# Weighting of the second map moved to GpSimd, and late value units and gate banks rearranged, in a two-block attention kernel

## The chip, the cores and the metric

The kernel runs on one core of a Trainium2 chip. The metric is the device time of one execution in microseconds, taken as the median of several runs. TensorE is called PE in the profile, VectorE DVE, ScalarE ACT, GpSimd POOL, SyncE SP.

## The reference, cut to what matters

Two transformer blocks run one after the other on 256 latent tokens of width 1024. The first block has a Fourier mixer layer, then a differential attention layer (8 heads of two maps, 512 keys: 256 latent and 256 context), each with a feed-forward part. The second adds 16 meta tokens and runs multi-head latent attention (MLA, 8 heads, 272 keys) and neighbourhood attention (NA, 16 heads) side by side, each times a silu gate, then one output projection.

```
differential:  p = softmax(q1 k1^T) - lam * softmax(q2 k2^T);   o = rmsnorm(p v) * gain;   x += gate * (o @ w_out)
MLA:           p = softmax(scale * (qn kn^T + qp kp^T));        y_mla = (p v) * silu(g_mla)
NA:            p = softmax(scale * q k_win^T + bias);           y_na  = (p v) * silu(g_na)
out:           x += concat(y_mla, y_na) @ w_out_2
```

## The kernel before, in words

Everything is fp32, kept exact to about fp32 by splitting each operand of a projection into a rounded part and a rest; a projection tile is then three fp32r matmuls per 128 rows of the contraction (`product`, lines 528 to 530, and for token-major tiles lines 966 to 968). SP loads weights by slabs of two halves; ACT rounds each half (line 503), DVE forms the rest (line 510), four halves fit. PE walks all projections as **units**: a unit is one PSUM bank, 24 matmuls for a contraction of 1024 and 6 for 256. A head unit is then squared by ACT, summed over partitions by PE (`unit_sum`) in bank 3 or 4, inverted by ACT (lines 1027 and 1029) and scaled by DVE (line 1128), with a rotation where needed (1143 to 1146); a token unit is copied out by ACT (line 1085); a meta unit (line 953) is added up by DVE (1107 to 1110). Units of the deep phases go round banks 0, 1, 2, 5, 6, 7 and are finished two units later; gate units go round banks 0, 1, 2. Each engine has its own instruction order written out by hand, and in-order waits on semaphores join them.

**Differential attention** (`att_pe`, `att_act`, `att_dve`) has 16 steps (8 heads, two query halves). Its first steps follow the last two token units of the phase: one is run before step 0, one in iteration 2. In iteration i, PE runs the scores of step i (line 1223, two maps, banks 0 to 3 in turn), in odd iterations the value product of a head (1238), in even ones the sum of squares of a head (1260), then the transposes of step i-2 (1252). ACT runs the two exponentials of step i (1277), copies the transposes of step i-2 out (1287), squares a head (1299) or forms its inverse root (1304, 1306). DVE takes the maxima of step i (1371), the reciprocals of the sums of step i-1 (1347), scales the second map (1353) and adds the scaled first one (1355), and in odd iterations scales a head (1382). POOL only rounds and splits the finished heads (`heads_split`, 1335 and 1337). Four parts of the output projection (15 matmuls each, contraction tiles 0 to 4 of output tiles 0 to 3) are run by PE after the transposes of iterations 17, 17, 19 and 20; the rest follows in `outproj_pe`, whose output tile 0 needs the last head's split (line 1328) for its contraction tile 7.

**MLA attention** (`mla_pe`, `mla_act`, `mla_dve`) has 8 steps of two heads: scores 1413 and 1417, maxima 1493, exponentials 1460, weights 1500, transposes 1428 and 1431 (bank 4 + step parity, and 7). Before it PE waits until all units of the phase, value tiles and their rests (line 1153) are out. **NA attention** (`na_pe`, `na_act`, `na_dve`) has 16 steps with scores 1580, transposes 1597 and 1600, and parts of the last projection (1547 to 1549) between. Of its last three units (two token units and one meta unit of the value matrix) only the meta unit is run in iteration 2.

Of the kernel before, what the change touches and what calls it, by code (L numbers as in the profile page):

```python
# [30 lines left out]
F32 = mybir.dt.float32  # L31
# [5 lines left out]
P = 128  # L37
# [154 lines left out]
def build(nc, d, out):  # L192

    with ExitStack() as ctx:
# [245 lines left out]
        s_hr = sem("head_rounded_by_pool")  # L440
        s_bias = sem("bias_ready")
# [430 lines left out]
        DIFF_UNITS[-2]["bank"], DIFF_UNITS[-1]["bank"] = 6, 5  # L872
        PHASES = [DIFF_UNITS, LAT_UNITS, GATE_UNITS, MLA_UNITS, NA_GATE_UNITS, NA_UNITS]
# [31 lines left out]
        for phase in PHASES:  # L905
            deep = phase in (DIFF_UNITS, MLA_UNITS, NA_UNITS)
            banks = (0, 1, 2, 5, 6, 7) if deep else (0, 1, 2)
            for i, u in enumerate(phase):
# [3 lines left out]
                last_in[u["bank"]] = u  # L912
        ROPED = [u for u in ALL_UNITS if u.get("rope")]
# [84 lines left out]
        def unit_sum(pe, u):  # L998

            h, m = u["h"], u["cols"]  # L1000
            o = ps[0:m, 3 + h % 2, 0:u["w"]]
# [19 lines left out]
        def unit_inverse(act, link, u):  # L1021
# [5 lines left out]
            link(nc.scalar.activation(inverse, ps[0:m, 3 + u["h"] % 2, 0:w], ACT.Ln,  # L1027
# [169 lines left out]
        def bank_free(pe, units, bank):  # L1197

            for u in [u for u in units if u["bank"] == bank][-1:]:
                if u["kind"] == "head":  # L1200
                    pe.wait_ge(s_unrm, u["h"] + 1)
                else:
                    pe.wait_ge(s_ucp, u["c"] + 1)
            for u in [u for u in units if u["kind"] == "head" and 3 + u["h"] % 2 == bank][-1:]:
                pe.wait_ge(s_unrm, u["h"] + 1)

        def att_pe(pe, a, tail, last_unit):

            for i in range(a["steps"] + 6):
                if i == 2:  # L1210
                    last_unit()
                if i < a["steps"]:
# [12 lines left out]
                    ins.then_inc(s_sc, 1)  # L1225
                if i % 2 == 1 and 0 <= (i - 5) // 2 < a["heads"]:
# [16 lines left out]
                if 2 <= i < a["steps"] + 2:  # L1243
                    j0 = i - 2
                    pe.wait_ge(s_w, a["s0"] + j0 + 1)
                    if j0 == 0:
                        bank_free(pe, DIFF_UNITS[:-1], 4)
                    if j0 == 1:
                        pe.wait_ge(s_ucp, 16)
                    positive(pe, s_trc, a["s0"] + j0 - 1)  # L1250
                    for j, (at, n) in enumerate(chunk_plan(a["keys"])):
                        ins = nc.tensor.transpose(ps[0:n, 4 + j0 % 2, j * P:(j + 1) * P],
                                                  a["ex"][:, j0 % a["deep"], 0, at:at + n], T["ident"])
                    ins.then_inc(s_tr, 1)
                if tail:
                    tail(i)
# [1777 lines left out]
```

## Time and profile before

| | |
|---|---|
| median of 3 runs | 1194.96 us (1193.94 to 1195.08) |
| the profiled execution: time | 1191.34 us |
| the profiled execution: span | 1189.6 us, 18840 instructions |
| mean granted TensorE clock | 0.995 |
| PE busy | 1150.6 us (97%) |
| DVE busy | 740.7 us (62%) |
| ACT busy | 556.5 us (47%) |
| POOL busy | 130.9 us (11%) |

The span goes from the first to the last instruction; the execution's own time is 1.7 us longer. A busy PE is not PE at its peak, since the ends of matmuls are modelled. The slot of one instruction is better read as the distance of the starts of two neighbours. The differential attention lies at about 623 to 684 us of the span, the MLA gates at 905 to 937, the MLA units at 937 to 994 and its attention to 1033, the NA attention at 1105 to 1155.

### The profile page before, as it was taken

Reading aid. Unit: us, or ns where it says so; the run is one execution under the profiler, and the core shown is the slowest. Engines: PE = TensorE matmul, PEld = TensorE weight load, DVE = VectorE, ACT = ScalarE, POOL = GpSimd, SP = SyncE. Lnnn points to the kernel's source line nnn. Section 1 sums busy time; section 2 is a strip of 40 time slices with the busy share of each in tenths; the row PEclk is TensorE's granted clock in tenths of the full one; section 3 lists DMA queues with packets and bytes.
Section 4 is the critical chain, followed back from the end, with each engine's and each line's share of the span. In section 5 each row is a group of like instructions: output and inputs, shape, how many; then the busy total and the mean of one; then the engine's idle time right before and its main releaser. Section 6 shows DMA issues by size and latency. Waiting matters only on the chain.

```text
span 1189.6 us, 18840 instructions
## 1 busy us (share of the span) xinstructions
PE 1150.6 (97%) x7088; PEld 966.6 (81%) x7088; DVE 740.7 (62%) x1236; ACT 556.5 (47%) x1058; POOL 130.9 (11%) x185
## 2 busy tenths in 40 slices
PE   8999999999999999999998999999999999999898
PEld 6665787877878888778995799999998887899666
DVE  5764566766733333578769696445568596645773
ACT  4453322222223232456447675444556676567662
POOL 0012011122200000212100110000010000132410
PEclk8999999999999999999999999999999999999999
DMA  8999356578732332223340155555553444164320
GB/s 281 376 336 323 130 163 195 170 252 278 263 107 72 107 106 72 70 72 106 107 143 1 36 173 182 182 195 188 176 152 107 139 145 133 53 200 142 110 72 35
DMA packets 121672, 182.85 MB, mean 154 GB/s; under 512 B 4497, under 2 KB 92896, under 8 KB 121600
## 3 DMA queue, kind: packets, MB, share of 16 engines
q1 hardware_dynamic: 113888, 154.44, 39.4%
q0 software_dynamic: 7712, 27.43, 7.1%
q8 instruction: 47, 0.77, 0.3%
q14 instruction: 25, 0.20, 0.1%
HBM read 180.48 MB, written 1.05 MB: 153 GB/s over the span
## 4 chain that ended last, share of the span: by engine, by line
PE 80%; DVE 10%; ACT 5%; issue 4%; POOL 1%; DVEq 0%; ACTq 0%; POOLq 0%
PE ps L528 20%; PE ps L530 20%; PE ps L529 20%; PE ps L966 2%; PE ps L968 2%; PE ps L967 2%; DVE wl L510 2%; PE ps L2607 1%; ACT wh L503 1%; DVE hl L737 1%; DVE nrm L721 1%; PE ps L2975 1%; PE ps L2977 1%; PE ps L2976 1%; PE ps L1223 1%
## 5 line engine op out<-in xcount | busy, mean ns | idle before, releaser
L510 DVE TENSOR_TENSOR wl<-raw,wh 128x1024 fp32r<-128x1024 f32 (+1 forms) x246 | 297.5, 1214 | 224.2 <-ACT wh L503 221.1
L528 PE MATMUL ps<-hh,wh 128*128 128x256 f32 (+3 forms) x1272 | 418.0, 329 | 7.6 <-DVE hl L737 2.8
L529 PE MATMUL ps<-hl,wh 128*128 128x256 f32 (+3 forms) x1272 | 414.0, 325 | 0.0
L530 PE MATMUL ps<-hh,wl 128*128 128x256 f32 (+3 forms) x1272 | 413.1, 325 | 0.0
L503 ACT ACTIVATE wh<-raw 128x1024 fp32r<-128x1024 f32 (+1 forms) x246 | 252.5, 1032 | 261.2 <-PE ps L530 249.6
L528 PEld LDWEIGHTS ps<-hh,wh 128*128 128x128 f32 x1272 | 239.6, 188 | 47.6 <-issue 14.8
L530 PEld LDWEIGHTS ps<-hh,wl 128*128 128x128 f32 x1272 | 240.0, 189 | 21.0
L529 PEld LDWEIGHTS ps<-hl,wh 128*128 128x128 f32 x1272 | 239.0, 188 | 20.2
L528 PE MATMUL ps<-ah,wh 128*128 128x256 f32 (+2 forms) x376 | 126.1, 335 | 2.7 <-DVE big L1128 1.5
L529 PE MATMUL ps<-al,wh 128*128 128x256 f32 (+2 forms) x376 | 124.2, 330 | 0.0
L530 PE MATMUL ps<-ah,wl 128*128 128x256 f32 (+2 forms) x376 | 124.2, 330 | 0.0
L528 PEld LDWEIGHTS ps<-ah,wh 128*128 128x128 f32 x376 | 70.6, 188 | 11.6 <-DVE big L1128 1.7
L529 PEld LDWEIGHTS ps<-al,wh 128*128 128x128 f32 x376 | 70.8, 188 | 7.1
L530 PEld LDWEIGHTS ps<-ah,wl 128*128 128x128 f32 x376 | 70.6, 188 | 7.3
L2375 DVE TENSOR_TENSOR al<-big,ah 128x512 fp32r<-128x512 f32 (+1 forms) x42 | 23.3, 558 | 81.3 <-ACT ah L2038 81.3
L2038 ACT ACTIVATE ah<-big 128x512 fp32r (+3 forms) x42 | 21.8, 524 | 103.4 <-PE ps L530 103.4
L966 PE MATMUL ps<-wh,hh 128*128 128x256 f32 x192 | 54.8, 285 | 3.2 <-DVE wl L510 1.6
L968 PE MATMUL ps<-wh,hl 128*128 128x256 f32 x192 | 53.9, 281 | 0.0
L967 PE MATMUL ps<-wl,hh 128*128 128x256 f32 x192 | 53.9, 281 | 0.0
L761 POOL TENSOR_TENSOR big<-sq 128x512 f32<-128x512 f32 (+2 forms) x4 | 4.4, 1101 | 443.7 <-ACT sq L644 443.7
L1098 POOL TENSOR_TENSOR al<-sq,ah 128x256 fp32r<-128x256 f32 (+2 forms) x32 | 30.7, 960 | 143.7 <-ACT ah L1018 143.7
L1128 DVE SCALAR_TENSOR_TENSOR big<-ps,par,rstd 128x256 f32<-128x256 f32 (+3 forms) x60 | 22.6, 405 | 32.3 <-ACT rstd L1029 32.2
(298 smaller groups left out, 1530.6 us busy)
## 6 DMA issues: line engine op xcount, KB each, us to landing
raw<-in_ffn_w_in SPq DMA_DIRECT2D x44, 1024.0 KB, 5.2
raw<-in_ffn_w_out SPq DMA_DIRECT2D x22, 1024.0 KB, 5.0
raw<-in_w_in SPq DMA_DIRECT2D x22, 1024.0 KB, 5.4
big<-in_w_ada SPq DMA_DIRECT2D x16, 1024.0 KB, 10.6
big<-in_w_ada POOLq DMA_DIRECT2D x24, 512.0 KB, 4.5
ex<-in_w_ada POOLq DMA_DIRECT2D x24, 512.0 KB, 5.1
raw<-in_diff_w_in SPq DMA_DIRECT2D x12, 1024.0 KB, 5.2
raw<-in_w_out SPq DMA_DIRECT2D x8, 1024.0 KB, 5.0
```

The lines of the kernel that those rows point to most:

```text
L503: ins = nc.scalar.activation(place(wh), v, ACT.Copy)
L510: ins = nc.vector.tensor_tensor(place(wl), v, place(wh).bitcast(F32), ALU.subtract)
L528: nc.tensor.matmul(o, w_hi, m_hi, start=first, stop=False, **kw)
L529: nc.tensor.matmul(o, w_hi, m_lo, start=False, stop=False, **kw)
L530: return nc.tensor.matmul(o, w_lo, m_hi, start=False, stop=last, **kw)
L966: nc.tensor.matmul(oo, mh[:, k, tok], cols(wh), start=first, stop=False)
L967: nc.tensor.matmul(oo, mh[:, k, tok], cols(wl), start=False, stop=False)
L968: ins = nc.tensor.matmul(oo, ml[:, k, tok], cols(wh), start=False, stop=last)
L1098: nc.gpsimd.tensor_tensor(al[:, h % 2, 0:w], sq[:, h % 2, 0:w], ah[:, h % 2, 0:w].bitcast(F32), ALU.subtract).then_inc(s_ulow, 1)
L1128: ins = nc.vector.scalar_tensor_tensor(out=dst, in0=o[:, a:b], scalar=par_of(u["gain"])[0:m, :], in1=inverse_of(u)[:, a:b], op0=ALU.mult, ...
L2038: nc.scalar.activation(ah[:, at % 2, 0:n], big[:, bass.ds(k * n, n)], ACT.Copy)\
L2375: nc.vector.tensor_tensor(al[:, at % 2, 0:n], big[:, bass.ds(k * n, n)], ah[:, at % 2, 0:n].bitcast(F32), ALU.subtract).then_inc(s_as, 1)
```

## The change

Four things are done. (1) Differential attention: the scaling of the second map goes from DVE to POOL (`second_maps` takes the place of `heads_split` and does its work too); the two-map sum on DVE, the transposes and their copies come one iteration later; on PE the transposes stand ahead of the value product, on ACT the copies ahead of the exponentials; two token units are late (iterations 2 and 3); the four parts of the projection stand in iterations 16 to 19, ahead of the value product or the sum. (2) MLA gates use five banks. (3) MLA: the last three value units (128, 128 and 16 tokens) are run in iteration 2 of the attention on PE, ACT and DVE, with the round and the split of the next weight half behind them; the one big wait ahead of the attention becomes waits per bank and per head; the banks of the sums are swapped. (4) NA: two late units (token and meta) instead of one, sums swapped. The two new semaphores are `s_rc` and `s_second_map`.

```diff
+        for u, bank in zip(MLA_UNITS[-3:], (7, 6, 5)):
+            u["bank"] = bank
...
-            banks = (0, 1, 2, 5, 6, 7) if deep else (0, 1, 2)
+            banks = (0, 1, 2, 5, 6, 7) if deep else (0, 1, 2, 6, 7) if phase is GATE_UNITS else (0, 1, 2)
...
+                if u["kind"] == "head":
+                    u["sum"] = 3 + (u["h"] + (phase in (MLA_UNITS, NA_UNITS))) % 2
...
         def att_pe(...):
-                if i == 2:
-                    last_unit()
+                if i in (2, 3):
+                    late_unit(i - 2)
...
+                if 3 <= i < a["steps"] + 3:
+                    j0 = i - 3
+                    pe.wait_ge(s_w, a["s0"] + j0 + 1)
...
+                    ins.then_inc(s_tr, 1)
+                tail(i)
                 if i % 2 == 1 and 0 <= (i - 5) // 2 < a["heads"]:
...
-                if 2 <= i < a["steps"] + 2:
-                    j0 = i - 2
...
-                if tail:
-                    tail(i)
...
         def att_act(...):
-                if i == 2:
-                    units_act(act, link, last_unit, False)
+                if i in (2, 3):
+                    units_act(act, link, DIFF_UNITS[i - 4:][:1], False)
...
+                if 3 <= i < a["steps"] + 3:
+                    j0 = i - 3
...
+                if i < a["steps"]:
+                    for c in range(a["maps"]):
+                        act.wait_ge(s_mx, a["s0"] + i + 1)
...
+        def second_maps(pool, a):
+
+            for i in range(a["steps"] + 8):
+                if i < a["steps"]:
+                    j = i % a["deep"]
+                    pool.wait_ge(s_rc, i + 1)
+                    part = a["ex"][:, j, 1, 0:a["keys"]]
+                    nc.gpsimd.tensor_scalar(part, part, rc[:, j, 1:2], sml[:, 5:6], ALU.mult, ALU.mult)\
+                        .then_inc(s_second_map, 1)
+                f, odd = divmod(i - 6, 2)
+                if odd and 0 <= f < a["groups"] - 1:
+                    pool.wait_ge(s_on, a["g0"] + f + 1)
+                    nc.gpsimd.tensor_copy(o_out(a, f, hh), o_scaled(a, f)).then_inc(s_hr, 1)
...
         def att_dve(...):
-                    link(nc.vector.tensor_scalar(exp[:, j, 1, 0:n], exp[:, j, 1, 0:n], rc[:, j, 1:2], sml[:, 5:6],
-                                                 ALU.mult, ALU.mult))
...
+                if 1 <= i <= a["steps"]:
...
+                    nc.vector.reciprocal(rc[:, j, 0:a["maps"]], sm[:, j, 0:a["maps"]]).then_inc(s_rc, 1)
+                if 2 <= i <= a["steps"] + 1:
+                    j = (i - 2) % deep
+                    dve.wait_ge(s_second_map, i - 1)
+                    nc.vector.scalar_tensor_tensor(out=exp[:, j, 0, 0:n], in0=exp[:, j, 0, 0:n],
+                                                   scalar=rc[:, j, 0:1], in1=exp[:, j, 1, 0:n],
+                                                   op0=ALU.mult, op1=ALU.add).then_inc(s_w, 1)
...
         def mla_pe(pe, tail):
+            heads = [u for u in MLA_UNITS if u["kind"] == "head"]
+            late = MLA_UNITS[-3:]
             for i in range(MLA_STEPS + 4):
+                if i == 2:
+                    units_pe(pe, late)
                 if i < MLA_STEPS:
                     f, t = divmod(i, 2)
+                    if i < 2:
+                        for b in (2 * i, 2 * i + 1):
+                            bank_free(pe, MLA_UNITS[:-3], b)
+                    pe.wait_ge(s_urdy, heads[3 * f + 2]["r"] + 1)
+                    pe.wait_ge(s_unrm, heads[12 + 2 * f + 1]["h"] + 1)
...
         mla_act:
+                if i == 2:
+                    units_act(act, link, MLA_UNITS[-3:])
...
         mla_dve:
             for i in range(MLA_STEPS + 6):
+                if i == 2:
+                    units_dve(dve, link, mark, MLA_UNITS[-3:])
                 if i < MLA_STEPS:
                     dve.wait_ge(s_sc, MLA_S0 + i + 1)
...
         na_pe:
                 if i == 2:
-                    units_pe(pe, NA_UNITS[-1:])
+                    units_pe(pe, NA_UNITS[-2:])
...
         diff_tail:
-                for m in {steps + 1: (0, 1), steps + 3: (2,), steps + 4: (3,)}.get(i, ()):
-                    pe.wait_ge(s_ex, ATT["diff"]["maps"] * steps)
+                m = i - steps
+                if 0 <= m < 4:
+                    pe.wait_ge(s_ex, ATT["diff"]["maps"] * (steps - 1 + m // 2))
                     outproj_part(pe, diff_out[m], m, range(5), L, head_split)
...
-            units_pe(pe, GATE_UNITS, before=1)
+            units_pe(pe, GATE_UNITS[:3], before=1)
+            pe.wait_ge(s_rstd, ORDER.index("lat") + 1)
+            units_pe(pe, GATE_UNITS, before=3)
...
-            units_pe(pe, MLA_UNITS)
-            pe.wait_ge(s_urdy, ROPED[-1]["r"] + 1)
...
-            pe.wait_ge(s_vlow, 8)
+            units_pe(pe, MLA_UNITS[:-3])
...
-            units_act(act, link, NA_UNITS[:-1])
+            units_act(act, link, NA_UNITS[:-2])
```

The lists of units that PE, ACT and DVE run ahead of each attention are shortened in the same way everywhere.

## Rows read from the trace of the kernel before

**Rows 1.** A stretch of plain projections: busy time of each engine and, last, clock and DMA
```profile
1045.00:1100.00 55.00, 55.00 (x454) 55.00 (x453) 30.28 (x41) 38.94 (x78) 13.35 (x18) 1.00 0.51 159
```

**Rows 2.** What PE waited for in the differential attention, 622 to 684 us
```profile
PE ps L1260 <- ACT sq L1299: 3.1, 5, 1.2
PE ps L1252 <- DVE big L1355: 1.9, 2, 1.1
```

**Rows 3.** Timeline of PE, one pair of steps: start, us, what, [idle before]
```profile
641.33 1.13 PE L1223 MATMUL ps<-big 64*128 64x512 f32 x4
642.39 1.99 PE L1238 MATMUL ps<-x_ctx,big 128*128 128x256 f32 x8
644.22 0.60 PE L1252 MATMUL ps<-tab,big 128*128 128x128 f32 x4
644.75 1.13 PE L1223 MATMUL ps<-big 64*128 64x512 f32 x4
646.03 0.70 PE L1260 MATMUL ps<-sq,tab 128*128 128x256 f32 x2
...
647.10 1.13 PE L1223 MATMUL ps<-big 64*128 64x512 f32 x4
```

**Rows 4.** Timeline of DVE, one step of the same stretch
```profile
642.51 1.23 DVE L1371 TENSOR_REDUCE nm<-ps 128x2 f32<-128x1024 f32 x1 [0.34 <-PE ps L1223]
...
643.84 0.55 DVE L1353 TENSOR_SCALAR big<-big,rc,sml 128x512 f32<-128x512 f32 x1
644.42 0.75 DVE L1355 SCALAR_TENSOR_TENSOR big<-big,rc 128x512 f32<-128x512 f32 x1
```

**Rows 5.** Groups of POOL instructions by form: count, busy us, mean ns, idle before
```profile
L761 POOL TENSOR_TENSOR big<-big,sq 128x512 f32<-128x512 f32 x8 | 10.7, 1340 | 18.7 <-ACT sq L644 18.2
L1335 POOL CAST hh<-nrm 128x256 fp32r<-128x256 f32 x7 | 2.8, 396 | 55.8 <-DVE nrm L1382 55.8
```

**Rows 6.** Timeline: GpSimd ahead of VectorE
```profile
669.76 0.80 POOL L1337 TENSOR_TENSOR hl<-nrm,hh 128x256 fp32r<-128x256 f32 x1
669.99 1.11 DVE L1355 SCALAR_TENSOR_TENSOR big<-big,rc 128x512 f32<-128x512 f32 x1
```

**Rows 7.** Timeline: VectorE ahead of GpSimd
```profile
320.67 1.23 DVE L510 TENSOR_TENSOR wl<-raw,wh 128x1024 fp32r<-128x1024 f32 x1 [1.68 <-ACT wh L503]
321.08 0.96 POOL L1901 CAST half_r<-tab 128x128 fp32r<-128x128 f32 x1
```

**Rows 8.** Timeline: first maxima and third scores of the differential attention
```profile
624.62 1.23 DVE L1371 TENSOR_REDUCE nm<-ps 128x2 f32<-128x1024 f32 x1
...
627.84 1.13 PE L1223 MATMUL ps<-big 64*128 64x512 f32 x4
```

**Rows 9.** Timeline: last sum of squares, and the product behind the last head
```profile
680.30 0.59 PE L1260 MATMUL ps<-sq,tab 128*128 128x256 f32 x2
...
683.40 0.19 PEld L528 LDWEIGHTS ps<-hh,wh 128*128 128x128 f32 x1 [0.24 <-DVE hl L1328]
```

**Rows 10.** Timeline: the MLA gates' weight splits and the fourth gate unit
```profile
920.27 1.23 DVE L510 TENSOR_TENSOR wl<-raw,wh 128x1024 fp32r<-128x1024 f32 x1
...
923.03 0.36 PE L528 MATMUL ps<-hh,wh 128*128 128x256 f32 x1 [2.25 <-ACT big L1085]
...
923.94 1.23 DVE L510 TENSOR_TENSOR wl<-raw,wh 128x1024 fp32r<-128x1024 f32 x1 [0.98 <-ACT wh L503]
```

**Rows 11.** Timeline: start of the MLA attention, PE's first scores, DVE's split and maxima
```profile
995.55 1.16 PE L1413 MATMUL ps<-big 128*128 128x272 f32 x4 [1.69 <-DVE mv_low L1153]
...
995.96 1.23 DVE L510 TENSOR_TENSOR wl<-raw,wh 128x1024 fp32r<-128x1024 f32 x1 [0.56 <-ACT wh L503]
...
1001.28 0.72 DVE L1493 TENSOR_REDUCE nm<-ps 128x2 f32<-128x544 f32 x1 [0.54 <-PE ps L1417]
```

**Rows 12.** Timeline: start of the NA attention, ACT's last token copy, PE's second scores
```profile
1105.79 0.38 ACT L1085 ACTIVATE big<-ps 128x256 f32<-128x256 f32 x1 [2.11 <-PE ps L968]
...
1107.97 0.59 PE L1580 MATMUL ps<-big 64*128 64x192 f32 x4 [1.71 <-DVE big L1128]
```

More of the change, by code:

```diff
@@ L1000, in unit_sum @@
             h, m = u["h"], u["cols"]
-            o = ps[0:m, 3 + h % 2, 0:u["w"]]
+            o = ps[0:m, u["sum"], 0:u["w"]]
             if "low" in u:
@@ L1026, in unit_inverse @@
             inverse = inverse_of(u)
-            link(nc.scalar.activation(inverse, ps[0:m, 3 + u["h"] % 2, 0:w], ACT.Ln,
+            link(nc.scalar.activation(inverse, ps[0:m, u["sum"], 0:w], ACT.Ln,
                                       bias=eps_c[0:m, 0:1], scale=1.0 / u["dim"]))
@@ L1201, in bank_free, with att_pe @@
                     pe.wait_ge(s_unrm, u["h"] + 1)
+                elif "vlow" in u:
+                    pe.wait_ge(s_vlow, u["vlow"] + 1)
                 else:
                     pe.wait_ge(s_ucp, u["c"] + 1)
-            for u in [u for u in units if u["kind"] == "head" and 3 + u["h"] % 2 == bank][-1:]:
+            for u in [u for u in units if u["kind"] == "head" and u["sum"] == bank][-1:]:
                 pe.wait_ge(s_unrm, u["h"] + 1)
-        def att_pe(pe, a, tail, last_unit):
+        def att_pe(pe, a, tail, late_unit):
             for i in range(a["steps"] + 6):
-                if i == 2:
-                    last_unit()
+                if i in (2, 3):
+                    late_unit(i - 2)
                 if i < a["steps"]:
@@ L1366, in att_dve @@
                     dve.wait_ge(s_sc, a["s0"] + i + 1)
-                if 1 <= i <= a["steps"] and not diff:
-                    inverted = inverse(i - 1)
-                if i < a["steps"]:
                     b = score_bank(a, i, 0)
@@ L1422, in mla_pe @@
                     pe.wait_ge(s_w, MLA_S0 + j0 + 1)
+                    if j0 == 0:
+                        bank_free(pe, MLA_UNITS[:-3], 4)
+                        pe.wait_ge(s_vlow, late[0]["vlow"] + 1)
+                    if j0 == 1:
+                        pe.wait_ge(s_ucp, late[2]["c"] + 1)
                     if j0 >= 2:
@@ L1435, in mla_pe @@
                     pe.wait_ge(s_trc, MLA_S0 + 2 * f + 2)
+                    if f == 0:
+                        pe.wait_ge(s_vlow, late[1]["vlow"] + 1)
+                        pe.wait_ge(s_meta, 3)
                     if f >= 1:
```

94 lines of the change are left out of this document (34 added, 60 removed).

## The prediction

> **What bounds the kernel now.** I read first a stretch of plain projections, then the waits of PE, then the timelines of the four places that the change touches. In a plain stretch PE is busy all 55.00 us with 454 matmuls at a granted clock of 1.00, the 2.4 GHz level [rows 1]. A 256-column matmul so takes a slot of 0.12 us, a unit of 24 takes 2.9, and the stretch can't be shortened by any reordering. Only where PE stands idle is there anything to win. In the differential attention PE waited 3.1 us for the squares of a head (5 times) and 1.9 us for the weights (2 times), 5.0 in all [rows 2]. One pair of steps takes 5.77 us from scores to scores (641.33 to 647.10). Its parts by the distances of starts: scores 1.06, value product 1.83, transposes 0.53, scores 1.06 again, sum of squares with transposes 1.07, so 5.55 of work and 0.22 idle [rows 3]. DVE's step is 1.33 from the maxima to the second map's scaling, 0.58 to the two-map sum, and 0.75 for that, 2.66; two steps are 5.3, and a head's scaling, also of one product over 256 columns, adds about 0.5: 5.8 [rows 4]. **DVE and PE are nearly level there**: the most that a free DVE gives is PE's idle time.
>
> **Sum for the differential attention, steps between.** Without the scaling, DVE needs 2 x 2.08 + 0.5 = 4.7 per pair and bounds no more. The tightest path is then from the scores of an even step to the transposes of the step two before: 1.18 until the maxima start [rows 3, 4], 1.33 until the two-map sum starts (it now stands where the scaling stood), 0.75 for it, 3.3 in all. PE has by then run scores, transposes, sum of squares and scores, 3.2. Some 0.1 stays idle per pair. Of the 3.1 us of waits for squares, the longest, 1.2, is at the end [rows 2]; 1.9, and 0.3 of slack in the modelled ends, lie between. They fall to 0.4: **-1.8**. The longer way from exponential to transposes (one more iteration) and the copies ahead of the exponentials cost nothing: the exponentials then end about 3 us after their scores started, and PE comes back to that bank 5.5 us after. The cover would be gone if ACT were late by 2 us.
>
> **The second map on POOL.** The trace has no scaling there. A cast of 256 columns takes 0.40, so one input of 512 some 0.8; two inputs of 512 take 1.34 [rows 5]. I take 0.8, since the operation has one tensor input, as the cast. It is needed one DVE step later, 2.1 us at the least. What it does to DVE hangs on who starts first. Where a POOL subtraction started 0.23 ahead, the two-map sum took 1.11 instead of 0.75, and ended 0.54 after POOL's end [rows 6]. Where DVE started first it took its usual 1.23 and the POOL cast, of only 128 columns, took 0.96 and ended 0.14 after DVE [rows 7]. In the new order the reciprocal releases POOL through a semaphore, while DVE goes on with the sum of the step before; I take DVE to be first. POOL then waits 0.75 and works 0.8, 1.6 of the 2.1: **0**; with 1.34 it is 2.1, just enough. The Trainium skill (SBUF — State Buffer, section SBUF: two separate sides) states that the pair of ports shared by the two is locked for a whole instruction by whichever starts first, and that the other blocks; both pairs of rows agree. By that rule a sum of DVE that comes second would wait up to a whole scaling, which is the first rival below.
> The two head operations (0.4 and about 0.75) follow the scaling of an odd step and end 2.8 after its reciprocal, so they delay the two-map sum of the other parity by 0.6, which has some 1 us of slack: 0. POOL's wait for a finished head, with the next scaling queued behind it, is met by then, since DVE scales that head an iteration earlier. No DMA issue is moved on any queue.
>
> **Its start.** DVE's first maxima start at 624.62, because DVE is in the rotation of the last head until then; that chain isn't changed. Before, a token unit stood between second and third scores, and these ran at 627.84 [rows 8]. Now two units leave the path ahead, so first and second scores are 2.9 us earlier, one unit follows, and PE then waits for the first exponentials: maxima 1.23, two exponentials 1.4, so third scores at 627.4 after 2.5 us of idling. The second late unit comes behind them, the fourth scores at 631.4, and the second and third transposes wait 0.5 and 0.3 for DVE. Idle so far 3.3, where before 2.0 (the 1.9 of [rows 2]): **+1.2**, bounds 0 and +2.5.
>
> **Its end.** From the last sum of squares to the product behind the last head's split lie 3.1 us (680.30 to 683.40), of which PE idled only 0.24 [rows 9], since the fourth part (15 matmuls, 1.8) and 6 matmuls (0.7) stood between. Now all four parts stand ahead; only the 0.7 is left: 2.1 idle. The last sum also waits for the square of a value product that has only just ended, 0.6. Gone are the 1.2 and the 0.24: **+1.3**, bounds 0 and +2.5. So the differential attention comes out at -1.8 + 1.2 + 1.3 = **+0.7**.
>
> **Gates.** The fourth gate unit started at 923.03 after waiting 2.25 for ACT's copy [rows 10]. With bank 6 it needs only its weights, ready at 920.27 + 1.23 = 921.5. But the fifth needs the next split, from 923.94 to 925.17, where it used to start at 923.03 + 2.9 = 925.9: **-0.7**, and never beyond -2.25.
>
> **MLA.** PE waited 1.69 for the value tiles' rests, and the first scores ran at 995.55 [rows 11]. Without three value units ahead, ACT inverts the last head without copies between, and the first scores, which need that head's bank, start about 1.0 earlier; PE idles 2.5 there. Then iteration 2. Before, round (1.06, in ACT's timeline) and split (995.96, 1.23 long) of the next half were over before the first maxima. Now they come behind both first exponentials and ACT's three copies, and **DVE takes them ahead of the third maxima**. Work: second maxima at 998.0, exponentials until 999.8, copies 1.2, round 1.06, split 1.23: third maxima at 1003.2, where they were at 1001.28 [rows 11]. Behind them wait the third exponentials, the first copy of the transposes, and so the weights and transposes of the third step: **+2.0**. Nothing gives it back, since PE is full from there to 1018. Bounds: -1.7, if the late units only fill the idle time, and +2.3, round and split in full.
>
> **NA.** ACT waited 2.11 for a token unit before it inverted the last head, and PE's second scores 1.71 for that head [rows 12]. Now the head comes at once and the swapped sum bank frees the second scores. But PE runs two late units (2.9 + 1.0) before the third scores, which come only 0.3 earlier; DVE, full from there on, gets to the fourth maxima 0.8 earlier: **-0.8**, bounds -2.1 and 0.
>
> **Sum**: +0.7 - 0.7 + 2.0 - 0.8 = +1.2 on the profiled execution's 1191.34, so 1192.5. The runs shown have a median of 1194.96, 3.6 above that execution; on it, **1196.2 us**. No change is within 0.2%, 2.4 us, about what a measurement of this kernel can tell.
>
> **Rivals.**
> - *POOL gets to the ports first* (slower). Decides: whether the scaling starts before DVE's sum. For it: POOL's semaphore wait may be short against DVE's own. Against: DVE has nothing to wait for there, and rows 7 show it keeping its time. The sum takes 0.36 more [rows 6], on the tight path once per pair and twice at the start, 7 or 8 times: +2.7; with a whole 0.8 each time, +6. Time 1199, at most 1202. Chance 0.2.
> - *The late value units fill PE's idle time in MLA* (faster). Decides: whether third maxima come before 1001.28. For it: 2.5 us of idling ahead of the scores and none of the late work on PE's own path. Against: the order on DVE, split first. Then -1.7 in place of +2.0: 1192.5. Chance 0.15.
> - *PE's idle time in the differential attention goes nearly whole*, start and end hidden too: -4 in place of +0.7, 1191.5. Against: the 3.1 chain behind the last head has no cover. Chance 0.05.
> - My own case, stalls moved rather than removed, has 0.6, its own range 1193.5 to 1199; 0.12 of it lies above +2.4, 0.03 below -2.4.
> Faster 0.15 + 0.05 + 0.03 = 0.23, slower 0.2 + 0.12 = 0.32, no change 0.45. The range 1192.0 to 1199.6 leaves out the worse half of the first rival and the last one.
>
> **What would show it.** Right: pair of 5.6 to 5.7, two-map sum 0.75 and POOL's scaling stretched to about 1.5; some 2.5 idle ahead of third scores at 627.4; a PE wait of 2 us for line 1328's successor; fourth gate at 921.5; third MLA maxima 1.5 to 2 late against the first scores' old place; fourth NA maxima earlier by 0.8. Wrong: two-map sums of 1.1, no wait behind the last head, or MLA maxima that don't wait for a split.

## The result, and the profile after

| | before | after |
|---|---|---|
| median, first comparison | 1194.15 us (1190.26 to 1195.08, 8 runs) | 1199.72 us (1198.51 to 1201.48, 8 runs) |
| ratio | | 1.0056 [1.0042, 1.0070] |
| the profiled execution: time, span, clock | 1191.34, 1189.6, 0.995 | 1199.98, 1198.2, 0.991 |

The kernel is slower, by more than the 0.2% that can be told: +5.6 us by these medians, where +1.2 was forecast. 1199.72 lies 0.1 us beyond the range of 1192.0 to 1199.6. The line numbers have moved: L530 to L532 are the old L528 to L530, L1231 the old L1223 (scores), L1243 the transposes, L1259 the value product, L1267 the sum of squares, L972 to L974 the token units.

The page's first lines:

```profile
span 1198.2 us, 18855 instructions
...
PE 1154.9 (96%) x7088; PEld 968.7 (81%) x7088; DVE 732.1 (61%) x1220; ACT 557.2 (47%) x1058; POOL 150.9 (13%) x201
...
PEclk8999999999999999999999899999999999999999
```

DVE lost 9 us of work and POOL took 20. PE runs the same 7088 matmuls, but is busy 4.3 us longer, and one slice of the clock row, beside the first, has an 8. Both say that part of the loss is not waiting.

**Where it went, by stage.** Both kernels issue the same number of matmuls, so the start of PE's n-th matmul in one can be set against the n-th in the other. Taken outside the reordered places, the lag (start in the changed kernel less start in the kernel before) tells by its growth over a stage what that stage cost. The numbers are 3000 and 3600 around the differential attention, 5100 and 5400 around the gates, 5700 and 6100 around MLA, 6600 and 6850 around NA's start, 6850 and 7000 around NA's end; a kernel with added matmuls is shifted by their count.

| run (all against the first profile of before) | start | diff. att. | gates | MLA | NA start | NA end | in all |
|---|---|---|---|---|---|---|---|
| my terms | | +0.7 | -0.7 | +2.0 | -0.8 | 0 | +1.2 |
| after | -0.95 | **+7.54** | -0.64 | +1.98 | -0.95 | +1.59 | +8.58 |
| after, second profile | -2.35 | +7.31 | -0.62 | +2.03 | -0.95 | +1.58 | +6.98 |
| before, second profile | -0.34 | -0.01 | 0.00 | +0.01 | -0.01 | -0.01 | -0.35 |

Three of my four terms stand within 0.15 us. NA's end has a clock drop, for which I had nothing (+1.6). The differential attention is off by 6.8.

**What PE waited for in it**, the changed kernel's waits from 616 to 700 us (us in total, times, longest):

```profile
PE ps L530 <- POOL hl L1352: 3.5, 1, 3.5
PE ps L1231 <- ACT big L1299: 2.3, 1, 2.3
PE ps L530 <- DVE hl L1335: 1.8, 1, 1.8
PE ps L1267 <- ACT sq L1306: 0.5, 1, 0.5
PE ps L1243 <- DVE big L1374: 0.4, 1, 0.4
```

In all 8.5 us, against 5.0 [rows 2] and 0.24 [rows 9]: 3.3 more. The second, third and fourth are the waits that I had put at 2.5, 2.1 and 0.6. The first I did not have at all. And 3.3 is not 7.5; the rest is the clock, in the table by windows (busy time and count of PE, PEld, DVE, ACT, POOL, then the granted clock, DMA share, GB/s):

```profile
624.00:626.40 2.40, 0.11 (x1) 0.00 (x0) 2.02 (x3) 1.48 (x5) 0.00 (x0) 1.00 0.00 0
...
627.70:630.40 2.70, 2.70 (x14) 2.70 (x13) 1.95 (x3) 1.60 (x6) 1.19 (x1) 0.50 0.00 0
...
668.80:672.40 3.60, 0.14 (x3) 0.02 (x1) 3.29 (x3) 1.71 (x3) 3.45 (x3) 0.88 0.00 0
672.40:678.00 5.60, 5.60 (x24) 5.31 (x25) 0.96 (x2) 1.42 (x3) 1.13 (x2) 0.50 0.59 190
```

PE idles for nearly all of 624.0 to 626.4 and of 668.8 to 672.4. Behind both it runs at 0.50, the 1.2 GHz level: 24 matmuls fill 5.60 us.

**The steady pair is a little shorter than forecast.** PE's timeline: 5.49 us from scores to scores (5.6 to 5.7 foretold), no idle time, where it was 5.77 [rows 3]; the last two rows stand behind the two waits at the stage's end:

```profile
639.36 1.13 PE L1231 MATMUL ps<-big 64*128 64x512 f32 x4
...
644.85 0.70 PE L1231 MATMUL ps<-big 64*128 64x512 f32 x2
...
672.39 0.58 PE L530 MATMUL ps<-hh,wh 128*128 128x256 f32 x1 [3.46 <-POOL hl L1352]
...
689.96 0.39 PE L530 MATMUL ps<-hh,wh 128*128 128x256 f32 x1 [1.80 <-DVE hl L1335]
```

**The wait that I had not seen**, DVE's and POOL's timelines at the end of the steps:

```profile
663.73 0.73 DVE L1374 SCALAR_TENSOR_TENSOR big<-big,rc 128x512 f32<-128x512 f32 x1
...
665.80 1.00 DVE L1374 SCALAR_TENSOR_TENSOR big<-big,rc 128x512 f32<-128x512 f32 x1
666.73 0.47 DVE L1382 SCALAR_TENSOR_TENSOR nrm<-ps,subg,rstd 128x256 f32<-128x256 f32 x1
667.89 0.17 DVE L1370 RECIPROCAL rc<-sm 128x2 f32<-128x2 f32 x1 [0.69 <-ACT big L1299]
667.97 0.73 DVE L1374 SCALAR_TENSOR_TENSOR big<-big,rc 128x512 f32<-128x512 f32 x1
669.11 2.64 DVE L512 TENSOR_TENSOR wl<-raw,wh 128x1024 fp32r<-128x1024 f32 x2 [0.41 <-ACT wh L505]
671.67 1.21 DVE L1374 SCALAR_TENSOR_TENSOR big<-big,rc 128x512 f32<-128x512 f32 x1
```

```profile
663.91 1.19 POOL L1345 TENSOR_SCALAR big<-big,rc,sml 128x512 f32<-128x512 f32 x1 [1.96 <-DVE rc L1370]
...
668.16 1.19 POOL L1345 TENSOR_SCALAR big<-big,rc,sml 128x512 f32<-128x512 f32 x1 [0.71 <-DVE rc L1370]
669.29 1.38 POOL L1350 CAST hh<-nrm 128x256 fp32r<-128x256 f32 x1
670.76 1.57 POOL L1352 TENSOR_TENSOR hl<-nrm,hh 128x256 fp32r<-128x256 f32 x1
```

The fifth head is normalised at 667.20. POOL is free from 667.45, but its queue holds the last scaling ahead of the head's cast, and that waits for a reciprocal until 668.06. The scaling ends at 669.35. By then DVE is in its two weight splits, and cast and subtraction take 1.38 and 1.57, where the ones before them took 0.39 and 0.73 (0.40 in [rows 5]). At these shorter durations the split would have ended at about 670.5 instead of 672.33; so, by my estimate, some 1.8 us of the wait come from DVE's work beside them and the rest from the scaling that stands ahead in POOL's queue. PE stands at the first projection part's fifth K tile from 668.9 to 672.4. The same rows show that POOL never got ahead of DVE's sum in the way of my first rival: the sum at 663.73 has its own 0.73, and the scaling beside it is stretched to 1.19. Only in odd steps, where a head's subtraction is under way on POOL, does the sum take 1.00, and the pair of steps is 5.49 even so.

### The profile page after: what moved, and what is told of

Read it like the earlier page. It is cut to its first block, busy times and chain, and to the rows that moved or that the text cites. A ratio compares the mean times of both kernels' runs of the same rounds, so it can differ in the third digit from the quotient of the medians.

```text
span 1198.2 us, 18855 instructions
## 1 busy us (share of the span) xinstructions
PE 1154.9 (96%) x7088; PEld 968.7 (81%) x7088; DVE 732.1 (61%) x1220; ACT 557.2 (47%) x1058; POOL 150.9 (13%) x201
## 4 chain that ended last, share of the span: by engine, by line
PE 80%; DVE 10%; ACT 6%; issue 3%; POOL 1%; DVEq 0%; ACTq 0%; POOLq 0%
PE ps L530 20%; PE ps L532 19%; PE ps L531 19%; DVE wl L512 2%; PE ps L972 2%; PE ps L973 2%; PE ps L974 2%; ACT wh L505 1%; PE ps L2628 1%; DVE hl L739 1%; PE ps L1231 1%; DVE nrm L723 1%; PE ps L1259 1%; PE ps L2994 1%; PE ps L2996 1%
## 5 line engine op out<-in xcount | busy, mean ns | idle before, releaser
L530 PE MATMUL ps<-hh,wh 128*128 128x256 f32 (+3 forms) x1272 | 419.4, 330 | 12.0 <-POOL hl L1352 3.5
L532 PE MATMUL ps<-hh,wl 128*128 128x256 f32 (+3 forms) x1272 | 413.9, 325 | 0.0
L530 PEld LDWEIGHTS ps<-hh,wh 128*128 128x128 f32 x1272 | 240.4, 189 | 52.4 <-issue 13.3
L532 PEld LDWEIGHTS ps<-hh,wl 128*128 128x128 f32 x1272 | 240.8, 189 | 20.9
L530 PE MATMUL ps<-ah,wh 128*128 128x256 f32 (+2 forms) x376 | 126.1, 335 | 2.7 <-DVE big L1134 1.5
L532 PE MATMUL ps<-ah,wl 128*128 128x256 f32 (+2 forms) x376 | 124.2, 330 | 0.0
L530 PEld LDWEIGHTS ps<-ah,wh 128*128 128x128 f32 x376 | 70.6, 188 | 11.6 <-DVE big L1134 1.7
L532 PEld LDWEIGHTS ps<-ah,wl 128*128 128x128 f32 x376 | 70.6, 188 | 7.3
L972 PE MATMUL ps<-wh,hh 128*128 128x256 f32 x192 | 55.7, 290 | 3.3 <-DVE wl L512 1.7
L974 PE MATMUL ps<-wh,hl 128*128 128x256 f32 x192 | 54.4, 283 | 0.0
L972 PEld LDWEIGHTS ps<-wh,hh 128*128 128x128 f32 x192 | 36.8, 191 | 7.1 <-issue 4.1
```

The source lines that it names most:

```text
L530: nc.tensor.matmul(o, w_hi, m_hi, start=first, stop=False, **kw)
L532: return nc.tensor.matmul(o, w_lo, m_hi, start=False, stop=last, **kw)
L972: nc.tensor.matmul(oo, mh[:, k, tok], cols(wh), start=first, stop=False)
L974: ins = nc.tensor.matmul(oo, ml[:, k, tok], cols(wh), start=False, stop=last)
```

## Experiments

All are made from the changed kernel unless said. The kernel before was measured beside each group; ratios are to that. Its medians there: 1191.81 (23 runs) for the first four, 1191.20 for the next four, 1191.58 and 1191.46 for the last two groups.

### 1. The head split ahead of the last scaling

```diff
 second_maps, i = 15:
-    scaling of step 15; cast and subtraction of head 4
+    cast and subtraction of head 4; scaling of step 15
```

> The changed kernel with one thing swapped: in the last odd step of the differential attention POOL splits the finished head (cast and subtraction) ahead of the scaling of the last second map, not behind it. Theory (POOL's queue holds the head back): the head is normalised at 667.2 and POOL's scaling before ends at 667.45, so the split is over by 668.8, about when the first projection part needs it. PE's wait of 3.46 us ahead of the fifth K tile falls under 0.5, and with it the granted clock of 0.50 behind it (5.6 us at half speed, worth 2.6): about -6, so 1193.7 us. Rival (DVE's two weight splits of 1.23 us block POOL's ports, whatever its order): the wait stays above 2 us and the time within 1.5 us of 1199.7. Second rival (clock drop not tied to the wait): -3.4 alone, 1196.3, with 0.50 still granted near 672.

Measured: 1194.14 us (1193.19 to 1196.17), ratio 1.0021 [1.0010, 1.0032]; differential attention +1.03 instead of +7.54, **-6.5**. The row "L530 <- POOL" is gone from the waits, and 671 to 678 runs at 1.00; the drop at the start stays (0.50 from 628.3 to 631.0). The forecast of 1193.7 holds, and both rivals fall. What is left behind the sixteenth scores is +1.6, near the +1.3 that the prediction had for the end. POOL's and DVE's timelines of this run, together:

```profile
668.45 0.74 POOL L1356 TENSOR_TENSOR hl<-nrm,hh 128x256 fp32r<-128x256 f32 x1
669.18 3.34 POOL L1345 TENSOR_SCALAR big<-big,rc,sml 128x512 f32<-128x512 f32 x1
...
668.54 1.20 DVE L1380 SCALAR_TENSOR_TENSOR big<-big,rc 128x512 f32<-128x512 f32 x1
669.69 2.36 DVE L512 TENSOR_TENSOR wl<-raw,wh 128x1024 fp32r<-128x1024 f32 x2
672.56 0.75 DVE L1380 SCALAR_TENSOR_TENSOR big<-big,rc 128x512 f32<-128x512 f32 x1 [0.51 <-POOL big L1345]
```

So DVE does hold POOL up: the scaling, 0.77 alone, starts while DVE's sum is still running, takes 3.34 and ends 0.47 behind the second split, and DVE then waits 0.51 for it. It costs PE nothing here, since what waits for it comes later. With the order in POOL's queue put right, DVE's splits alone made no wait for PE; in the changed kernel the two came together.

### 2. Both late units ahead of the third scores

```diff
-                if i in (2, 3):
-                    late_unit(i - 2)
+                if i == 2:
+                    late_unit(0)
+                    late_unit(1)
```

> The changed kernel with both late token units of the differential attention ahead of the third scores, where one now stands behind them. Theory (PE idles 2.3 us there because one unit covers too little, and then pays at half clock): third scores at 626.9 instead of 626.4, fourth at about 628 to 628.5 instead of 632.0, some of it given back at the second and third transposes, which wait for DVE's weights; the granted clock stays at 1.00. Net -2 to -3.5, so 1196.2 to 1197.7 us. Rival (DVE's chain of maxima, exponentials and weights sets the start, so that PE only waits elsewhere): the waits move to the transposes and the time stays within 1 us of 1199.7.

Measured: 1196.79 us, ratio 1.0038 [1.0024, 1.0053]; differential attention +4.18, **-3.4**. Relative to the first scores, the third now come at 7.8 (7.3 before the edit) and the fourth at 8.8 (12.9). The wait for exponentials falls from 2.3 to 0.2, transposes wait 1.2, and 622 to 630 has a clock of 1.00. The 3.5 wait for POOL at the end stays and is followed by 0.53.

### 3. The same waits, filled with idle work

```diff
 ahead of the third scores:
+    18 matmuls of 256 columns into the next late unit's bank
 first projection part, ahead of K tile 4:
+    27 matmuls of 256 columns into the second part's bank
```

> The changed kernel with idle work for PE: 18 matmuls of 256 columns into the bank of the next late unit ahead of the third scores (2.1 of the 2.3 us idle), and 27 into the bank of the next projection part ahead of its fifth K tile (3.2 of 3.46 us). Their results are written over, nothing waits for them, no wait is removed. Theory (the time behind the two stretches is TensorE's clock, and it fell because PE had idled): granted clock 1.00 behind both, the late unit takes 2.9 instead of 4.3 us and the stretch 672.4 to 678 takes 2.9 instead of 5.6: -3.5 to -4.5 in all, 1195.2 to 1196.2 us. Rival (the clock falls for another reason, or the slow stretch is slack): time as the changed kernel's, within 1 us of 1199.7, or 0.50 granted all the same.

Measured: 1197.20 us, ratio 1.0043 [1.0028, 1.0058]; differential attention +3.33, **-4.2** in the stage, as forecast. PE's rows of the two fills, and the windows behind them:

```profile
623.74 2.32 PE L2907 MATMUL ps<-wh,hh 128*128 128x256 f32 x18
...
667.04 3.39 PE L2898 MATMUL ps<-hh,wh 128*128 128x256 f32 x27
670.75 0.35 PE L530 MATMUL ps<-hh,wh 128*128 128x256 f32 x1 [0.33 <-POOL hl L1352]
```

```profile
627.26:630.20 2.94, 2.94 (x26) 2.87 (x24) 1.95 (x3) 1.95 (x7) 1.19 (x1) 1.00 0.00 0
670.75:676.00 5.25, 5.25 (x37) 4.89 (x38) 0.89 (x2) 1.63 (x4) 1.13 (x2) 1.00 0.63 200
```

PE still can't go on before 670.75, but it isn't idle meanwhile, and the clock stays at the 2.4 GHz level. By the ratio the whole kernel gained 1.6 us against the unedited kernel's 1.0056, or 4.3 against its 1.0079 (experiment 7). 1197.20 is above the forecast: in this profile the clock fell at MLA's start instead (MLA +4.86), which the fourth experiment takes up. So 3.3 us more waiting and 4.2 us of clock make the +7.5.

### 4. The old differential attention, all else changed

```diff
 att_pe, att_act, att_dve, heads_split, diff_tail and the unit lists: as in the kernel before
```

> The changed kernel with the whole differential attention as it was before (order, second map on DVE, one late unit, projection parts at their old places); gates, MLA and NA as changed. Theory (by the traces' lags between equal matmul numbers the differential attention costs 7.5 us, gates -0.6, MLA +2.0, NA -1.0): +0.4 over the kernel before, so 1194.0 to 1195.2 us. Rival (my own terms +0.7 for the differential attention, the rest lost to something between): 1199 us.

Measured: 1193.91 us, ratio 1.0010 [1.0000, 1.0021], by which it is +1.2 where +0.4 was forecast; differential attention +0.02. So the loss lies in the new differential attention and nowhere between, and the rival (1199) falls. But MLA is +5.08 here. In the changed kernel and in this one PE waits 2.13 us ahead of MLA's first scores. Windows of the wait and behind it, first of the changed kernel, then of this one:

```profile
998.00:1000.50 2.50, 0.41 (x2) 0.00 (x0) 1.29 (x5) 1.71 (x4) 0.00 (x0) 1.00 0.04 12
1000.50:1006.00 5.50, 5.47 (x32) 3.82 (x33) 2.39 (x6) 2.12 (x9) 0.00 (x0) 1.00 0.00 0
```

```profile
991.00:993.40 2.40, 0.34 (x2) 0.00 (x0) 1.24 (x5) 1.65 (x4) 0.00 (x0) 0.94 0.01 3
993.40:999.00 5.60, 5.53 (x14) 2.98 (x14) 0.87 (x3) 1.05 (x4) 0.00 (x0) 0.50 0.00 0
```

The same wait, once followed by 1.00 and once by 0.50, which costs 3 us. Experiments 1, 2 and 5 had no drop there, 3, 4 and 9 had one, and 8 had half of one (MLA +3.63). The Trainium skill (TensorE: Matmul & The Clock Gate, section What's actually happening) states that activity releases the throttle on the array's clock, and that the number of slow matmuls at the start of one and the same kernel varies from run to run. These rows agree, and show such chance in the middle of a kernel too.

### 5. MLA: the split behind the third maxima

```diff
 mla_dve, i = 2:
-    late units with the split of the next half; maxima
+    late units; maxima; the split of the next half
```

> The changed kernel with one split moved: in MLA's third iteration DVE splits the next half of weights behind the third maxima instead of ahead of them. Theory (the third maxima wait for ACT's rounding and DVE's split, as the profile has it: 1007.03 + 1.06, then 1.23, maxima at 1009.26): the maxima start at about 1007.1, their exponentials 1.9 earlier, and of the +2.0 that MLA costs at least 1.2 goes. Time -1.2 to -2.0 against the changed kernel. Rival (PE's late value units are the cost, three units of work that no longer hide anything): maxima earlier, but the lag of equal matmul numbers behind MLA stays within 0.5 us of +2.0.

Measured: 1197.78 us, ratio 1.0064 [1.0042, 1.0086] (the unedited kernel beside it 1.0079, below); MLA +1.17 instead of +1.98, **-0.8**, less than the 1.2 that the forecast had at the least and more than the 0.5 of its rival. The chain as it was (ACT's and DVE's timelines of the changed kernel), then DVE's with the edit:

```profile
1007.03 1.06 ACT L505 ACTIVATE wh<-raw 128x1024 fp32r<-128x1024 f32 x1
...
1008.12 1.23 DVE L512 TENSOR_TENSOR wl<-raw,wh 128x1024 fp32r<-128x1024 f32 x1 [1.08 <-ACT wh L505]
1009.26 0.72 DVE L1514 TENSOR_REDUCE nm<-ps 128x2 f32<-128x544 f32 x1
...
1010.09 0.73 DVE L1521 TENSOR_TENSOR ex<-ex,rc 128x544 f32<-128x544 f32 x1
```

```profile
1007.25 0.72 DVE L1514 TENSOR_REDUCE nm<-ps 128x2 f32<-128x544 f32 x1 [1.01 <-PE ps L1426]
1007.89 1.22 DVE L512 TENSOR_TENSOR wl<-raw,wh 128x1024 fp32r<-128x1024 f32 x1
...
1009.22 0.72 DVE L1526 TENSOR_TENSOR ex<-ex,rc 128x544 f32<-128x544 f32 x1
```

This kernel's first maxima lie 0.79 earlier on its clock (1001.67 against 1002.46), so the third come 1.2 earlier, and now wait for PE. But the second step's weights stand behind the split in either order, and gain 0.1. I had followed one of the two things that queue behind the split. The forecast of +2.0 for MLA was right by its own steps, though: round, split, maxima, at +2.0.

### 6. A version from the findings

```diff
+ the edits of experiments 1 and 2
- diff_tail: parts in iterations 16, 17, 18, 19
+ diff_tail: parts in iterations 16, 17, 18; part 4's K tiles 0, 1 in iteration 20 and 2 to 4 in 21
- MLA's late value units (MLA as before)
```

> A version from the findings: the changed kernel with the finished head split ahead of the last scaling on POOL, both late token units ahead of the third scores, the fourth projection part cut in two (six matmuls ahead of the last sum of squares, nine behind it, to cover the 0.6 and 2.0 us that PE waits for the last head), and MLA as it was before the change. Sum of the lags measured so far in the differential attention: +7.5 - 6.5 - 3.3 - 1.8 = -4.1 against the kernel before; gates -0.6, NA -1.0: -5.7 in all, ratio 0.995. Rival (the gains overlap: each removes a wait that the next one lets come back): between -2 and 0 against the kernel before.

Measured: **1186.74 us** (1185.52 to 1188.01, 11 runs), ratio 0.9959 [0.9946, 0.9973]: faster than both kernels. Differential attention -3.77 (forecast -4.1), gates -0.65, MLA -0.01, NA -1.00. Its waits there add to 2.2 (1.2 for weights, 0.8 for the last head, 0.2 for exponentials), against 5.2 in the kernel before. The gains nearly add up: the rival (-2 to 0) falls. NA's end is +1.54, a clock drop.

### 7. The changed kernel once more

> The changed kernel once more, unaltered, beside the others on their chip. Theory (its two clock drops in the differential attention belong to its long waits and come every time; those elsewhere come and go): granted clock 0.50 near 628 and 673 again, +6 to +8 against the kernel before. Rival (all drops come and go): one of the two is missing from this profile.

Measured: 1200.53 us, ratio 1.0079 [1.0060, 1.0098]. Both drops of the differential attention are there again (0.54 in 625 to 628, 0.50 in 670 to 676), as they are in experiment 5; the one at NA's end too (+1.58). The stage is +7.31. So the part of the forecast on the clock holds; the whole is +9.3 by the medians, above the +6 to +8. The two ratios of one kernel differ mostly by the median of the kernel before, 1194.15 and 1191.20.

### 8. The second map back on DVE

```diff
 (from experiment 1) att_dve:
-                    dve.wait_ge(s_second_map, i - 1)
+                    dve.wait_ge(s_rc, i - 1)
+                    link(nc.vector.tensor_scalar(exp[:, j, 1, 0:n], exp[:, j, 1, 0:n], rc[:, j, 1:2], sml[:, 5:6],
+                                                 ALU.mult, ALU.mult))
 second_maps: only the heads
```

> The kernel of the first experiment with the second map scaled by DVE again, directly ahead of the two-map sum; the new order of transposes, exponentials and projection parts is kept, and POOL only splits the heads. Theory (DVE was level with PE, and POOL's share is what brings the pair of steps from 5.77 to 5.50 us): DVE's two steps are 5.3 plus 0.5 again, the pair 5.8, PE idle 0.3 in each of six pairs, and the chain to the transposes 0.75 longer at the start: +2 to +3.5 against the first experiment, 1196 to 1197.5 us where that has 1194. Rival (the new order alone does it, POOL is not needed): pair 5.5 to 5.55, time within 1 us of the first experiment.

Measured: 1199.75 us, ratio 1.0072 [1.0054, 1.0090]; differential attention +6.13, 5.1 above experiment 1, where +2 to +3.5 was forecast. PE's waits and DVE's timeline:

```profile
PE ps L1243 <- DVE big L1370: 4.5, 7, 1.0
```

```profile
653.86 1.23 DVE L1359 TENSOR_REDUCE nm<-ps 128x2 f32<-128x1024 f32 x1 [0.71 <-PE ps L1231]
...
655.07 0.53 DVE L1368 TENSOR_SCALAR big<-big,rc,sml 128x512 f32<-128x512 f32 x1
655.64 0.75 DVE L1370 SCALAR_TENSOR_TENSOR big<-big,rc 128x512 f32<-128x512 f32 x1
```

The pair is 6.08 us, more than my 5.8. DVE is not full but in a ring with PE: the transposes wait 1.0 for the sum, the next maxima wait 0.71 for scores behind those transposes. From the first to the sixteenth scores it lost 3.5 us; another 1.6 lie behind them, with a clock of 0.59 after the last head's wait, which experiment 1 did not have there. So POOL's share is what makes the new order pay; the order alone would be worse than the old one.

### 9. The second map scaled twice on POOL

```diff
 (from experiment 1) second_maps:
+                    nc.gpsimd.tensor_scalar(part, part, rc[:, j, 1:2], sml[:, 5:6], ALU.mult, ALU.mult)\
+                        .then_inc(s_once, 1)
+                    pool.wait_ge(s_once, i + 1)
```

> The kernel of the first experiment with the second map scaled twice on POOL (so that its output lacks the right weight of the second map); nothing else. It asks how much slack POOL's share has, which I had put at nothing to pay. Theory (POOL runs beside PE with room: 1.20 per step twice and 1.15 for the head's split, 3.6 in a pair of 5.5): with 0.8 to 1.2 more per step POOL is at 5.2 to 5.9 per pair, and in odd steps the split still stands ahead of the next scaling; the pair grows to 5.6 to 6.2 us, +1 to +5 in all. Rival (POOL is the bound already, its port waits hidden in its own durations): the pair grows by two whole scalings, to 7 us or more, +10. Rival two (slack enough): pair 5.50 as before.

Measured: ratio 1.0040 [1.0026, 1.0053]; the pair of steps stays at 5.49 to 5.50, so the second rival is right: POOL has room for another scaling per step. Its timeline:

```profile
648.46 1.19 POOL L1346 TENSOR_SCALAR big<-big,rc,sml 128x512 f32<-128x512 f32 x1 [1.23 <-DVE rc L1380]
649.74 0.77 POOL L1349 TENSOR_SCALAR big<-big,rc,sml 128x512 f32<-128x512 f32 x1
```

Only the ends pay, 2.4 us together: one more wait of 0.4 for weights at the start, and 1.6 for the fifth head's split, which has no other step to hide behind. That is the same place where the change itself failed.

### 10 to 14. Idle work in the waits outside the differential attention

Two kernels, the version of experiment 6 ("joined") and the kernel before, each with fills ahead of MLA's first scores and in the two waits behind NA's last scores; and a second look at the kernel before. Each fill writes a bank whose readers PE first waits for. The expectations put the waits at 1.85, 1.06 and 1.23 us; the profile's own idle times are 1.69, 0.90 and 1.07.

```diff
+ 13 matmuls of 256 columns ahead of MLA's first scores
+ 7 and 8 (later 2 and 2) of 256 columns in the waits behind NA's last scores
```

> The joined version with idle work for PE in three waits outside the differential attention: 13 matmuls of 256 columns ahead of MLA's first scores (where PE waits 1.85 us), 7 and 8 in the two waits behind NA's last scores (1.06 and 1.23); nothing waits for them. Theory (these waits are where the clock falls now and then, for about 1.5 us at NA and 3 at MLA): no granted clock under 1.00 behind them, -1.5 in the profiled span, median -0.5 to -2 against the joined version, spread of the runs no more than 2 us. Rival (the fill costs as much as it saves): within 0.5 us of the joined version.

> The kernel before with the same three fills. Its own runs fall in two groups, near 1190 us at a mean clock of 0.995 and near 1194.3 at 0.992. Theory (the upper group has a clock drop at MLA's or NA's wait): the fills leave the lower group alone, median 1189.5 to 1191, spread under 2.5 us. Rival (the drop is elsewhere, at the start of the kernel or in the differential attention): both groups stay.

> The kernel before, unaltered, for a second profile. Theory (drops outside the differential attention come and go): stages as long as in the first profile except where a clock drop follows MLA's or NA's waits; none in the differential attention, whose longest wait is 1.2 us. Rival: a drop in the differential attention here too.

Measured: 1189.59 us, ratio 0.9980 [0.9970, 0.9991], for the joined version, and 1195.78 us, ratio 1.0036 [1.0023, 1.0050], for the kernel before: both *slower* than without. The fill at MLA costs nothing (MLA +0.02 and -0.01); those at NA cost 4.23 in both:

```profile
1139.88 3.19 PE L1574 MATMUL ps<-big 128*128 128x256 f32 x14
```

Seven matmuls of plain fp32 stand as 14 in the profile and take 3.19 us, 0.46 each, in a wait of 0.90; an fp32r one of the same 256 columns took 0.13 in experiment 3. So the fill was too long. No 3 us window from 25 us to 1180 us is below 0.97 in either. The second look at the kernel before has every stage within some 0.01 of the first, which is what the method by matmul numbers can tell here, and no drop before its end. With shorter fills:

> The joined version with the fills of the tenth run cut to size: behind NA's last scores 2 and 2 matmuls instead of 7 and 8. Their operands there are plain fp32, so each ran as two passes of 0.226 us: 3.19 and 3.62 us in waits of 1.06 and 1.23. Theory (the oversize alone cost +4.25, and with the fill no clock drop comes at MLA or NA): last matmul 5.5 to 6 us ahead of the kernel before (lag without drops), median 1185 to 1186.5 where the joined version has about 1187. Rival (two short fills do not hold the clock): 0.50 again behind NA, as the joined version.

> The kernel before with the same fills cut to size. Theory (the upper of its two groups of runs, 1194.3 at a mean clock of 0.992, has a clock drop behind MLA's or NA's wait, and the fill takes that chance away at no cost): no run above 1193, median 1190 to 1191.3. Rival (the group comes from elsewhere): runs at 0.992 and 1194 remain.

Measured: the joined version **1184.78 us** (1183.62 to 1186.06), ratio 0.9942 [0.9926, 0.9959], last matmul 6.0 ahead, as forecast, and the median just under the forecast range; the kernel before 1190.72 us, ratio 0.9995 [0.9982, 1.0007], no gain that can be told. The same stretch behind NA's last waits, in the joined version and with the short fills:

```profile
1144.40:1147.40 3.00, 3.00 (x10) 2.44 (x11) 2.38 (x4) 2.92 (x7) 0.00 (x0) 0.51 0.88 337
```

```profile
1144.40:1147.40 3.00, 3.00 (x16) 2.14 (x16) 2.31 (x4) 2.39 (x6) 0.00 (x0) 1.00 0.82 325
```

Of the 17 runs of the kernel before beside these, five were at 1194.7 to 1195.1 us; with fills one of 12 was above 1193 (1193.81). That speaks for MLA's and NA's waits as the home of most of that group, but the counts are small, one run remains, and no profile has caught the kernel before in a drop there: this is likely, not shown. Nor do single profiles show that the fills held the clock at NA, since half of the profiles without a fill had no drop there either. Only the fills of experiment 3 stand in waits that were followed by a drop in every profile without them.

## Why the prediction was wrong, point by point

The +7.5 of the differential attention is +2.0 up to the seventh scores, -2.6 from there to the sixteenth, and +8.1 behind them, where +1.2, -1.8 and +1.3 stood.

- **Steps between** (-1.8): right, and a little more. The pair fell to 5.49 against 5.6 to 5.7 foretold; the way from the seventh to the sixteenth scores took 24.06 us instead of 26.66, -2.6.
- **POOL at 0**: right for the steps. The scaling is 0.77 alone (I took 0.8) and 1.19 beside DVE's sum, which keeps its 0.73; the doubled scaling shows the slack. **Wrong for the end.** The prediction followed POOL's queue "by then, since DVE scales that head an iteration earlier", that is, from the side of the head's arrival. It did not ask the reverse: in iteration 15 a finished head is queued *behind* a scaling whose reciprocal comes 0.9 us later, and part 1, moved up one iteration, needs that head at once. Experiment 1 undoes that order alone, and 6.5 us go.
- **Its end** (+1.3, bounds 0 and +2.5): this is the step that failed; it measured +8.1. I checked only the last of the four parts against what it waits for. The waits that I named came as sized (1.8 and 0.5 for 2.1 and 0.6). The one of 3.46 for the fifth head was missing, and so were the 2.7 us of slower clock behind it; they leave 2.0, inside the bounds. A part moved from iteration 17 to 16 is a consumer moved ahead of its producer.
- **Its start** (+1.2): right in its waits (2.31 for 2.5; third scores at 626.42, on the time axis of the kernel before 627.37, foretold at 627.4). The fourth scores were foretold at 631.4. With the idle work of experiment 3, which keeps the clock, they come at 631.4 on that axis; in the changed kernel at 633.0. Without the clock the start costs +0.5 up to the seventh scores (experiment 3), less than I had, with it +2.0: the term is near the result between two errors, too high in the waits and nothing for the clock.
- **The clock**: in no term and no rival, though 2.5 us of idling at the start stood in the text: this is the second thing that failed, a cost put at nothing. It is 4.2 us of the +7.5: 1.5 at the start, 2.7 at the end. The trace of before did not show it: its longest wait in the differential attention is 1.2, and a wait of 2.25 at the gates [rows 10] had a clock of 1.00 behind it, in all four profiles that have this wait. The length of a wait alone so doesn't tell whether the clock falls; what else does is open.
- **Gates** (-0.7): -0.64. The fourth gate unit starts at 928.17, which is 921.6 on the time axis of the kernel before (its lag there is 6.6), foretold at 921.5; PE then waits 0.55 for the split, as argued.
- **MLA** (+2.0): +1.98, by the chain foretold (rounding, split, third maxima); experiment 5 shows that the place of the split ahead of the maxima is 0.8 of it. **NA** (-0.8): -0.95.
- **Rivals**: POOL first did not happen for the scaling; only a head's subtraction came ahead of DVE's sum, in odd steps, and the pair stayed at 5.49. Its 1199 to 1202, which hit the measured time, would have been right for the wrong reason, and it is by this rival alone that the range reached within 0.1 us of the result: that is luck. The MLA rival fell: the third maxima moved +2.0. No rival had the cause.

Sum of the stages that come every time: +7.5 - 0.6 + 2.0 - 1.0 = +7.9, where I had +1.2. The medians gave +5.6 and +9.3, since the median of the kernel before itself moves by 3 us between comparisons.

## What to carry to other kernels

Where work is moved ahead by an iteration, take each of its inputs and ask which instruction *stands in the queue ahead of that input's producer* there, at the ends of the loop too. A wait on the matmul engine can have two prices, its length and a slower clock behind it: two waits of 2.3 and 3.5 us cost 4.2 us on top here. Where these waits stayed, idle matmuls into a free bank kept the clock (experiment 3), but take their durations from a trace: with plain fp32 operands one took 0.46 us, with fp32r ones 0.13.

## What the runs showed of the hardware that I had not expected

- A POOL operation beside DVE's two-input operations can be held for several of them in a row: in experiment 1 a scaling that takes 0.77 alone took 3.34, behind the end of a sum and two splits. In the changed kernel cast and subtraction ran beside the same two splits without being held for both, and these took 2.64 instead of 2.36. The Trainium skill (SBUF — State Buffer, section SBUF: two separate sides) states that the one that comes second blocks fully. The rows agree, and add that it may lose the next turns too.
- The clock fell behind waits of 0.90 and 1.07 us at NA's end, with 0.65 us of work between them (after, two profiles; experiments 1, 2, 6, 8), and did not behind the very same waits in others (experiments 3, 4, 5, 9; the kernel before, twice). A drop there costs about 1.6 us each time, one at MLA 1.6 to 3.1.
- Stages without a clock drop repeat within 0.06 us from profile to profile (MLA +1.98 to +2.03, NA's start -0.94 to -1.00), while medians of the same kernel moved by 3 between comparisons: a difference of one stage can be read from single traces where the whole time can't show it.
